# Two-layer encoder step: where the late conditioning pieces stand around the sample's queries and the first unit's attention

## What is computed

```python
for layer in range(DEPTH):
    mod = jax.nn.silu(c) @ ada_w[layer] + ada_b[layer]
    sh_m, sc_m, g_m, sh_f, sc_f, g_f = jnp.split(mod, 6, axis=-1)
    h = modulate(x, norm_mix_w[layer], sh_m, sc_m)
    ...  # layer 0: latent attention (MLA); layer 1: band attention
    x = x + g_m[:, None, :] * out
    h = modulate(x, norm_ffn_w[layer], sh_f, sc_f)
    x = x + g_f[:, None, :] * peer_ffn(h, p_w_q[layer], p_subkeys[layer], p_u[layer], p_v[layer])
    if layer == N_A - 1:
        k_new, v_new = shared_kv(x, c, kv_ada_w, kv_ada_b, kv_norm_w, w_kv, k_norm)
```

## Time and profile before

| what | value |
|---|---|
| median of 3 executions | 4176.54 us (4174.93 to 4184.52) |
| the profiled execution's own time | 4168.8 us |
| its span in the profile | 4166.9 us |
| mean granted TensorE clock | 0.802 of full speed |
| busy: PE, DVE, POOL, ACT | 63%, 59%, 59%, 11% |
| DMA, mean over the span | 355 GB/s |

### The profile page before, as it was taken

One profiled execution on the slowest core, in us unless ns is written; L12 is line 12 of the kernel. 1 busy time (PEld: TensorE's weight loads), 2 busy tenths in 40 slices (PEclk: granted clock), 3 DMA queues, 4 the chain that ended last, 5 costly groups with the idle time before them and its releaser, 6 DMA issues.

```text
span 4166.9 us, 31596 instructions
## 1 busy us (share of the span) xinstructions
PE 2633.7 (63%) x9649; PEld 958.8 (23%) x9649; DVE 2452.3 (59%) x5936; ACT 452.8 (11%) x1097; POOL 2448.0 (59%) x2323
## 2 busy tenths in 40 slices
PE   6587854664564455655465765656464677767789
PEld 2144532221222111211121222222121321111122
DVE  2119687786666556755773665677557667754410
ACT  2124411110010000110011011011001110000000
POOL 0000145777776757775676565556666677777776
PEclk8788866786787676767667877878686899999999
DMA  9761677999998999998998998899899999999999
GB/s 350 272 228 51 199 253 234 357 370 347 388 395 340 379 403 395 394 379 352 406 400 333 393 392 332 344 376 368 333 411 409 399 385 409 405 410 408 409 410 371
DMA packets 482966, 1478.16 MB, mean 355 GB/s; under 512 B 61568, under 2 KB 135248, under 8 KB 482128
## 3 DMA queue, kind: packets, MB, share of 16 engines
q0 software_dynamic: 332160, 1208.77, 75.0%
q1 hardware_dynamic: 125056, 255.33, 16.6%
q10 hardware_dynamic: 25584, 12.06, 1.0%
HBM read 1448.97 MB, written 28.57 MB: 355 GB/s over the span
## 4 chain that ended last, share of the span: by engine, by line
DMA 34%; POOL 23%; PE 18%; DVE 14%; issue 10%; ACT 1%; SPq 1%; ACTq 0%; DVEq 0%; POOLq 0%
DMA A<-in_uv,A 30%; POOL A L1930 12%; POOL A L1950 11%; PE P L939 8%; DVE A L1753 6%; DMA A<-in_ada_w 3%; PE P L847 2%; PE P L626 1%; PE P L881 1%; PE P L817 1%; PE P L687 1%; DVE A L1640 1%; DVE A L1637 1%; DVE A L1448 1%; PE P L804 1%
## 5 line engine op out<-in xcount | busy, mean ns | idle before, releaser
L939 PE MATMUL P<-A 128*32 128x512 f32 x4608 | 1314.2, 811 | 1185.5 <-DMA A<-in_uv,A 1117.5
L1930 POOL DMA_INDIRECT A<-in_uv,A x1152 | 1217.5, 1057 | 832.4 <-DVE A L1753 580.7
L1753 DVE CUSTOM_DVE_ANT_0 A<-A 128x1024 f32<-128x1024 f32 x900 | 1093.9, 1224 | 773.9 <-DMA A<-in_uv,A 766.4
L1950 POOL DMA_INDIRECT A<-in_uv,A x1152 | 1220.2, 1059 | 444.9 <-issue 320.2
L939 PEld LDWEIGHTS P<-A 128*32 128x32 f32 x4608 | 268.7, 132 | 2046.3 <-issue 1584.4
L1753 DVE CUSTOM_DVE_ANT_0 A<-P,A 128x1024 f32<-128x1024 f32 x252 | 307.8, 1224 | 263.0 <-DMA A<-in_uv,A 261.9
L956 PE MATMUL P<-A 128*128 128x512 f32 (+1 forms) x480 | 230.8, 627 | 18.5 <-DMA A<-in_w_kv 11.6
L817 PE MATMUL P<-A 128*128 128x128 f32 (+2 forms) x832 | 152.1, 317 | 87.1 <-DVE A L1603 82.6
L1961 POOL DMA_DIRECT2D out_ckv_p<-A x4 | 2.2, 548 | 333.9 <-DVE A L1528 333.9
L847 PE MATMUL P<-A 128*128 128x512 f32 (+1 forms) x320 | 190.9, 727 | 1.9 <-DMA A<-in_w_oA 1.3
L804 PE MATMUL P<-A 96*64 96x320 f32 (+9 forms) x320 | 148.5, 564 | 28.2 <-DMA A<-kBp_scratch 13.0
(11 more groups left out here) (177 smaller groups left out, 2127.5 us busy)
## 6 DMA issues: line engine op xcount, KB each, us to landing
A<-in_ada_w SPq DMA_DIRECT2D x28, 2048.0 KB, 9.3
A<-in_w_kv SPq DMA_DIRECT2D x80, 512.0 KB, 8.6
A<-in_uv,A POOLq DMA_INDIRECT x2304, 7.8
A<-in_w_oA SPq DMA_DIRECT2D x40, 512.0 KB, 7.0
A<-in_w_q SPq DMA_DIRECT2D x40, 512.0 KB, 8.2
A<-in_w_oB SPq DMA_DIRECT2D x40, 512.0 KB, 7.9
A<-in_p_w_q SPq DMA_DIRECT2D x2, 4096.0 KB, 15.8
G<-mod_scratch SPq DMA_DIRECT2D x8, 512.0 KB, 7.6
```

The costliest lines, as they stand in the source:

```text
L939: ins = pe.matmul(Y[32 * j:32 * j + 32, b, :], spread[:, w:w + STRIDE], row[:, 512 * b:512 * b + 512], start=(m == 0), stop=(m == STRIDE - ...
L1753: dve.tensor_tensor_reduce(u_slot[b], row, u_slot[b], 1.0, 0.0, ALU.mult, ALU.add, dots[u % 2][:, j:j + 1]).then_inc(sem("dots_done"), 1)
L1930: pool.indirect_dma_start(u_slot[at % U_SLOTS], None, table, bass.IndirectOffsetOnAxis(ap=expert[u % 2][:, j:j + 1], axis=0)).then_inc(sem ...
L1950: pool.indirect_dma_start(row, None, table, bass.IndirectOffsetOnAxis(ap=expertT[u % 3][:, n:n + 1], axis=0)).then_inc(sem(name), 16)
```

## The change

Two places are edited together. `RAMP` puts one late piece ahead of the turning of the sample's queries instead of six, two behind it instead of three, and thirteen inside attention instead of seven, the last six of them one after each of the steps a15 to a20. SP's program follows: five pieces (12 to 16) ahead of attention instead of eleven, pieces 17 and 18 behind values(0), and one piece behind out_rows(g) for g = 0 to 4 (19 to 23), three for g = 5 (24 to 26) and one for g = 6 (27). `pass_mods` for the groups 3 and 4 moves from g = 0 to g = 2, behind that turn's piece 21. No instruction is added or removed.

```diff
-RAMP = ["llllllQlll" + "aal" * 7 + "a" * 7, "spsssss", ...
+RAMP = ["lQll" + "aal" * 7 + "al" * 6 + "a", "spsssss", ...
@@ sync, ahead of attention
-            pieces(4 * EARLY, 4 * EARLY + 11)
+            pieces(4 * EARLY, 4 * EARLY + 5)
@@ sync, attention
                 keys(1)
                 values(0)
+                if u == 0:
+                    pieces(4 * EARLY + 5, 4 * EARLY + 7)
                 for g in range(C):
                     if g + 2 < C:
                         keys(g + 2)
...
                     out_rows(g)
-                    if u == 0 and g == 0:
+                    if u == 0 and g < C - 1:
+
+                        n = 4 * EARLY + 7
+                        pieces(*((n, n + 1), (n + 1, n + 2), (n + 2, n + 3), (n + 3, n + 4), (n + 4, n + 5), (n + 5, n + 8), (n + 8, n + 9))[g])
+                    if u == 0 and g == 2:
                         pass_mods(EARLY, EARLY + 2, "mods2")
                         biases_of_mods(EARLY + 2, ADA_GROUPS, "biases_loaded")
-                    if u == 0 and g < 5:
-
-                        pieces(4 * EARLY + 11 + g, 4 * EARLY + 12 + g)
```

More of the change, by code:

```diff
@@ L52 @@
 EARLY = 3
-RAMP = ["llllllQlll" + "aal" * 7 + "a" * 7, "spsssss", "ccp" * 8 + "e" + "ccp" * 7 + "cp" * 5 + "e" + "cp" * 3,
+RAMP = ["lQll" + "aal" * 7 + "al" * 6 + "a", "spsssss", "ccp" * 8 + "e" + "ccp" * 7 + "cp" * 5 + "e" + "cp" * 3,
         "bdp" * 9 + "bbd" * 6 + "t" + "rdddrdddrdddrdddrdddr", "kkddh" * 8 + "f" + "kkddh" * 8 + "kkkfddhkkk" + "hhhh"]
```

## The result

| | kernel before | changed kernel |
|---|---|---|
| median | 4175.74 us (4 runs, 4171.21 to 4184.52) | 4252.07 us (4 runs, 4245.57 to 4259.02) |
| ratio | | 1.018, 95% interval 1.0157 to 1.0204 |
| span of the profiled execution | 4166.9 us | 4243.5 us |

The change makes the kernel 76 us slower. The forecast was 4240, with a range of 4203 to 4275.

The account below looks back on a forecast made before the run. Loads bind ahead of attention, PE inside it. Start -35, exposed loads +74, six more pieces some 12, half clock the remaining 12: +63 us, 4232 on the profiled execution, 4240 on the median; range 4203 to 4275.

Parts of the forecast that it names:

- part 1: Ahead of attention: six of nine pieces leave the path, so attention starts at 167.2, 35.0 us earlier.
- each us costs one: Ahead of attention: each us that ACT's second store of the queries is late takes one us off the early start's gain.
- part 2: Inside attention: six pairs of heads each begin with an exposed key load, waits of 9.0, four times 8.7, and 14.7 us.
- part 3: Pairs inside attention: half clock after each long wait adds 2.9 us to 8.1, so 11.0 us a pair.
- the bound of 6.6: Pairs inside attention: upper bound in us of the half-clock addition, with the whole pair at half clock.
- the prediction's last sign: Changed trace, PE's gaps in attention: if the gaps fit and the sum doesn't, the clock is wrong.
- part 4: Attention's end, from a15: late values and output weights, then piece 27 and DVE's last sum, put the result at 341.3 us.
- Half clock throughout: Rival, inside attention: PE never gets its full clock back; +89 us, so 4265; chance 0.18.
- Short loads pass: Rival, DMA in attention: keys land some 4 us after a piece's end instead of 8.7; +25, so 4200; chance 0.09.
- Faster: Rival, inside attention: key loads are never late; -21 us, so 4156; chance 0.06.
- The start does not move: Rival, ahead of attention: keys(0) stays held near 193 us, the 35 us are lost, time 4275; chance 0.03.
- The long part: The gathers behind attention, untouched by the change: they move one for one with what the ramp gains or loses.

Follow-up runs that it names:

- e6: Kernel before with the sample's queries turned behind the first late piece instead of the sixth, nothing else; ratio to the kernel before 1.0010 (0.9989 to 1.0030).
- e1: Changed kernel with SP's loads issued ahead of the pieces' waits, thirteen pieces still inside attention; ratio to the kernel before 1.0002 (0.9981 to 1.0023).
- e2: Changed kernel with SP's waits kept, but keys, values and output weights issued ahead of the piece; ratio to the kernel before 1.0070 (1.0047 to 1.0093).
- e7: Changed kernel with the last piece (27) behind DVE's final attention step instead of ahead of it; one execution, 4403.07 us.
- e4: Changed kernel with eight extra resultless PE products ahead of the waits for keys(2) to keys(7); ratio to the kernel before 1.0154 (1.0126 to 1.0183).
- e9: Changed kernel with eleven extra resultless PE products ahead of the waits for keys(2) to keys(7); one execution, 4365.72 us, kernel before 4290.93.

## Why the prediction was right, point by point

- **The early start** (part 1), 35.0 us forecast: 35.4 measured. DVE's norm ran from 133.85 to 139.9 and the queries were turned at 144.88, behind piece 12. The second store took 11.8 us instead of 9.1 and held keys(0) to 159.0, 2.6 us behind piece 14's end. The wait for keys(0) was 8.64 all the same: piece 16, issued at 156.5, landed 7.4 us later, at 163.9, and the scores began 1.2 us behind that. So "each us costs one" was wrong for such a store; the piece ahead in the queue covered its lateness. The start is right, and e6 shows that turning the queries early does not bring it alone.
- **The exposed loads** (part 2), the step that decides: right in place and number, and in the size of four of the six. Six waits for keys, 58.5 us forecast and 58.0 measured. That the sums agree so closely is in part luck: the wait for keys(3) was 10.37 us instead of 8.7, as piece 19 was slow to land, and the one with `pass_mods` 12.98 instead of 14.7 (its terms make 14.8), as `pass_mods` was 0.5 us shorter and keys and queries were there 2.8 us behind it instead of 4.1, with the queue empty. So it is with the tail: values 8.5 instead of 10.4, output weights and a piece 6.3 and 1.3 instead of some 5 together. All waits of attention, 74 forecast, 74.1 measured. e1 shows that SP's order makes them, e2 that 5.6 of 8.7 us are queueing.
- **The half clock** (part 3) is the term that was mis-sized. I took 11.0 us for a pair with its piece, 2.9 over full clock, from the one stretch behind a wait of 9 us. Five pairs took 13.36, 13.44, 12.68, 13.43 and 12.70 us, 65.6 in place of 55: 5.1 each over the 8.02 of full clock, nearer to the bound of 6.6 that was the rival's than to 2.9. The two pieces and four steps ahead of them took 13.5 instead of 11.2, for the same reason. Together 12.9 us too little. With the tail 0.6 and the waits 0.5 shorter than forecast this is the whole difference between the 174.1 us that I had from first scores to the result and the 185.8 measured. It is what the prediction's last sign says: gaps fit and the sum doesn't, so the clock. The rows of before had the better price. I counted half clock up to 208 and no further, but in the same stretch a chunk ran at half clock again, with no wait between:

```profile
217.79 3.56 PE L847 MATMUL P<-A 128*64 128x512 f32 x4
```

The granted clock of that stretch, 0.77 over 19.5 us, makes 0.23 x 19.5 = 4.5 us lost behind the one wait of 9 us, and the pair from 242.79 stayed at half clock throughout.
- **The tail** (part 4): from a15's start to L1630 49.4 forecast, 48.8 measured. That DVE's last sum holds the result cost 3.6 us with its piece (e7 takes it away). That the last `pass_mods` is covered holds: the result to the first gather took 153.1 us, 152.7 before.
- **The rivals.** Half clock throughout (+89): between it and the forecast (+63) lie the +74.6 measured from piece 12 to the result. The five pairs had a clock of 0.55 to 0.59, so it was near the truth, but full clock did come back at the end of a pair (the piece at 243.79 took 1.92 us). Short loads pass: e2 speaks against it. Faster: the count it doubted was right. The start does not move: it moved by 35.4.
- **The long part** moved one for one with the ramp, as forecast: +0.4 and +3.4 us behind attention's result. (The prediction's reading of the page is one slice early: the DMA row has 7 in the seventh slice and 9 from the eighth on.)

## What to carry to other kernels

A queue whose program waits for free slots holds everything written behind that wait; when prefetches are reordered, compare for each load the moment it is issued with the moment it is wanted, not only the bytes. Put a short load that is wanted soon ahead of a long one in the same queue: here behind a piece of 2 MB it cost 8.7 us, ahead of it 3. And price a wait of TensorE with the half clock that comes after it, over the whole of the work up to the next wait and not only up to the first row at full clock: here 5 us on 8 us of work.

## What the runs showed of the hardware that I had not expected

The work right behind a wait is not the place to look for its price. In e2 the waits were only 2.9 to 3.1 us, and the first scores behind four of them still ran at full clock (0.75 us for two), but the output chunk of the same pair took 3.0 to 3.7 us instead of 1.9:

```profile
250.74 0.75 PE L813 MATMUL P<-A 96*64 96x320 f32 x2 [3.09 <-DMA A<-qA_scratch]
...
256.95 3.02 PE L856 MATMUL P<-A 128*64 128x512 f32 x4
```

How long an idle stretch brings the half clock these runs don't say. In e4 waits of 1.4 to 2.7 us stood ahead of pairs at 0.59 to 0.82, but behind one of 1.73 (297.10) every step ran at full clock; in e6 PE idled 2.06 and 1.80 us ahead of two pieces and kept a granted clock of 1.00 from 223.4 to 263.0; and in e9 the clock fell at 194.8 with no wait ahead.

And the same kernel took 4176, 4291, 4305 and 4307 us at four times. The 4305 and the 4291 are from one chip, so it is not the chip alone. Where the traces can be compared the ramp is equal to some 2 us, and the difference lies in the gathers; the cause is open.
